# Expert rows gathered as two half rows, one by token and one by slot, the second a tile later

## The reference

```
idx = ...                                   # (tokens, 8, 16) chosen by two top-k over product keys
g = jax.nn.softmax(top_s, axis=-1)
u = expert_down[idx]
act = jax.nn.gelu(jnp.einsum('thkd,td->thk', u, xb).astype(f32), approximate=False)
return jnp.einsum('thk,thkd->td', (g * act).astype(xb.dtype), expert_up[idx])
```

## Time and profile before

| | us |
|---|---|
| median of 3 runs | 4412.91 |
| lowest and highest run | 4394.77, 4413.0 |
| span of the profiled execution | 4384.4 |
| start of the first gather in it | 1435.3 |
| start of the last tile's copy of rows | 3969.1 |

### The profile page before, as it was taken

The page is one execution under the profiler, slowest core; times in us unless marked ns, Lnnn a source line. Parts: engine busy times, 40 slices in busy tenths (PEclk is TensorE's granted clock), DMA queues, the critical chain, the costliest instruction groups (busy, mean ns, idle before and its releaser), DMA issues.

```text
span 4384.4 us, 39661 instructions
## 1 busy us (share of the span) xinstructions
PE 3487.9 (80%) x11633; PEld 1922.7 (44%) x11633; DVE 2354.8 (54%) x4730; ACT 1050.6 (24%) x3019; POOL 1348.0 (31%) x1232
## 2 busy tenths in 40 slices
PE   7699996469997687786787788778769778877876
PEld 1698774135555342352353344335325324324432
DVE  0651111746663767457546646646755755664574
ACT  1110112123341222222222222222222222222222
POOL 0020110400000343344444443434444444443442
PEclk9799997689998898898899889889889889988988
DMA  7232210642323899999999999999999999999996
GB/s 273 69 103 110 82 61 31 246 165 86 101 72 134 345 374 374 381 384 366 361 389 368 376 375 379 366 370 380 382 384 378 381 374 383 377 375 375 395 382 272
DMA packets 210634, 1269.30 MB, mean 290 GB/s; under 512 B 25875, under 2 KB 51099, under 8 KB 74060
## 3 DMA queue, kind: packets, MB, share of 16 engines
q0 software_dynamic: 159504, 1114.68, 64.3%
q1 hardware_dynamic: 50902, 152.03, 9.9%
HBM read 1218.26 MB, written 48.36 MB: 289 GB/s over the span
## 4 chain that ended last, share of the span: by engine, by line
DMA 26%; PE 25%; issue 8%; ACT 4%; POOL 3%; DVE 3%; POOLq 0%; ACTq 0%; DVEq 0%; SPq 0%
DMA e_buf<-in_experts,e_idx 26%; PE ps L1771 22%; PE ps L1502 3%; POOL e_buf L1738 3%; DVE e_buf L1840 2%; ACT e_wts L1812 2%; ACT e_diag L1816 1%; ACT e_acts L1810 1%; DMA e_buf<-in_experts,e_idxT 0%; DMA r_wq<-in_w_query 0%; POOLq L58 0%; DVE r_work L1590 0%; DVE r_row L1591 0%; DVE r_work L1587 0%; DVE r_pos L1550 0%
## 5 line engine op out<-in xcount | busy, mean ns | idle before, releaser
L1771 PE MATMUL ps<-e_buf,e_diag 128*128 128x512 f32 x4096 | 2026.0, 652 | 638.7 <-ACT e_diag L1816 635.2
L1840 DVE SCALAR_TENSOR_TENSOR e_buf<-e_buf,e_h 128x1024 f32<-128x1024 f32 x1024 | 1248.2, 1227 | 1091.6 <-DMA e_buf<-in_experts,e_idx 1075.2
L1738 POOL DMA_INDIRECT e_buf<-in_experts,e_idx x1024 | 1195.4, 1167 | 1605.1 <-PE ps L1771 1406.3
L1771 PEld LDWEIGHTS ps<-e_buf,e_diag 128*128 128x128 f32 x4096 | 836.0, 210 | 1758.4 <-issue 990.9
L1810 ACT ACTIVATE e_acts<-e_dots 128x4 f32<-128x4 f32 x256 | 52.6, 205 | 2085.0 <-DVE e_buf L1840 2076.4
L1816 ACT ACTIVATE e_diag<-ident,e_wts 128x128 f32<-128x128 f32 x1024 | 327.3, 390 | 27.8 <-ACT e_wts L1812 2.7
L1502 PEld LDWEIGHTS ps<-r_h2T,r_wq 128*128 128x128 f32 x2304 | 269.3, 193 | 34.0 <-issue 34.0
L1502 PE MATMUL ps<-r_h2T,r_wq 128*128 128x128 f32 x2304 | 269.9, 276 | 3.1 <-DMA r_wq<-in_w_query 3.1
L830 PE MATMUL ps<-xo_w_out,xo_catT 128*128 128x512 f32 x512 | 224.5, 592 | 1.7 <-DVE xo_x L863 1.7
L1812 ACT ACTIVATE e_wts<-e_acts,e_gate 128x1 f32<-128x1 f32 x1024 | 218.5, 284 | 9.2 <-ACT e_acts L1810 1.1
L74 PE MATMUL ps<-p_wth,hT_high 128*128 128x512 f32 (+1 forms) x432 | 170.6, 395 | 10.9 <-PEq L413 10.9
(11 more groups left out here) (338 smaller groups left out, 3007.2 us busy)
## 6 DMA issues: line engine op xcount, KB each, us to landing
w_mod_sb<-in_w_mod SPq DMA_DIRECT2D x12, 2048.0 KB, 8.4
e_buf<-in_experts,e_idx POOLq DMA_INDIRECT x1024, 9.1
p_wt<-in_w_rows SPq DMA_DIRECT2D x6, 2048.0 KB
proj_d<-p_ev POOLq DMA_DIRECT2D x48, 256.0 KB, 2.3
x_zgv<-proj_d SPq DMA_DIRECT2D x8, 1536.0 KB
p_w<-in_w_chan SPq DMA_DIRECT2D x20, 512.0 KB, 4.3
r_wq<-in_w_query SPq DMA_DIRECT2D x4, 2048.0 KB, 20.2
xbc_d<-p_res POOLq DMA_DIRECT2D x12, 516.0 KB, 3.0
```

Of the source, the lines that this page charges most:

```text
L1738: return pool.indirect_dma_start(out=buf[s][:], out_offset=None, in_=io["experts"], in_offset=bass.IndirectOffsetOnAxis(ap=numbers, axis=0 ...
L1771: last = nc.tensor.matmul(g.bank(cols), diag[:, k % RING, :], buf[k % RING][:, D + cols * 512:D + (cols + 1) * 512], start=(k == 0), stop= ...
L1840: V.scalar_tensor_tensor(out=down, in0=down, scalar=1.0, in1=row, op0=ALU.mult, op1=ALU.mult, accum_out=out).then_inc(sem, 1)
```

## The change

The table `experts` becomes two tables, `expert_down` and `expert_up`, with rows of 4 KB. Each is fetched by its own gathers.

The down rows are fetched as before, a slot of 128 tokens at a time, into 7 buffers of 4 KB a partition. VectorE's dot is the same; a down buffer is free when its dot has ended.

The up rows are fetched a tile later and the other way round: one gather for each token, whose 128 slots lie on partitions. For this TensorE turns the indices and the gates of a tile (`turn_route`), VectorE copies them out (`keep_route`), TensorE turns the activations of the last tile (`turn_acts`), and VectorE multiplies gates and activations into `wz` (`weigh`), a zeroed tensor in which the weights of token t stand in column 32 t + 31, so that 32 neighbouring columns hold one token's weights at the right place and zeros elsewhere. TensorE then sums a token over partitions with 32 columns of weights (`add_up`). Four tokens of a group go to the four column groups of 32 (PSUM partitions 0, 32, 64, 96), two products of 512 columns for each. One signal `summed` a group frees its four buffers; there are 8 up buffers.

ScalarE's scaling and its diagonals go; it makes one gelu for half a tile. GpSimd issues down gather k of tile n and up gather k of tile n-1 in turn. So the first tile has down gathers alone, and a ninth turn has up gathers alone, with the 8 down and 8 up gathers of the sample rows. The finish of a tile comes two tiles after its dots. The loops over tiles are written out, the pieces of the routing are moved two groups later, and the waits on GpSimd are no longer kept apart with a nop of their own, except a few. Some constants of the phases before are freed to make room. The core of the diff:

```diff
-    def tensor(self, pe, n):
+    def tensor(self, pe, n, turned_kept=()):
 
         g, nc = self.g, self.g.nc
         pe.wait_ge(self.h2_in, n * 16 + 16)
+        for kept, count in zip(turned_kept, (n, n, n - 1)):
+            if count:
+                pe.wait_ge(kept, count)
...
+            if n and half == 0:
+                dve.wait_ge(route_ps, n)
...
-            V.tensor_copy(self.idx[:, ks], self.num[:, ks]).then_inc(self.numbered, 1)
+            V.tensor_copy(self.idx[n % 2][:, ks], self.num[:, ks]).then_inc(self.numbered, 1)
...
-PE_PIECES = {q: 1 for q in range(1, 14)}
-ACT_PIECES = {q: 1 for q in (2, 4, 6, 7, 9, 10, 12, 13, 14, 18, 26)}
-DVE_PIECES = {8: 2, 9: 3, 11: 2, 12: 3, 13: 2, 14: 2, 15: 2, 16: 2, 17: 4, 19: 4, 20: 4, 21: 3, 22: 3, 23: 3,
-              24: 3, 25: 3, 27: 1}
-
-FIRST_ACT_PIECES = {6: 1}
+PE_PIECES = {q: 1 for q in range(3, 16)}
+ACT_PIECES = {q: 1 for q in (4, 6, 8, 9, 11, 12, 14, 15, 16, 20, 28)}
+DVE_PIECES = {10: 2, 11: 3, 12: 2, 13: 3, 14: 2, 15: 2, 16: 2, 17: 2, 18: 2, 19: 4, 20: 4, 21: 4, 22: 3, 23: 3,
+              24: 3, 25: 3, 26: 3, 28: 1}
+
+FIRST_ACT_PIECES = {3: 1}
...
+        down = [sb(f"down{s}", [P, D]) for s in range(ND)]
+        up = [sb(f"up{s}", [P, D]) for s in range(NU)]
+        h2 = sb("h2", [P, D])
+        dots, acts = [sb(f"dots{b}", [P, SLOTS]) for b in range(2)], sb("acts", [P, SLOTS])
+        idxT, gateT = [sb(f"idxT{b}", [P, P], U32) for b in range(2)], [sb(f"gateT{b}", [P, P]) for b in range(2)]
+        wz = sb("wz", [P, Q * (P + 1)])
...
+            for n in range(NT):
                 sp.wait_ge(h2_kept, n + 1)
-                sp.dma_start(rt.h2[:], g.h2_d[bass.ds(n * P + P, P), :]).then_inc(rt.h2_in, 16)
-                if not first:
-                    store_y(n - 1)
-                sp.dma_start(fin.x1[:], g.x1_d[bass.ds(n * P, P), :]).then_inc(fin.x1_in, 16)
-
-            tile(0, True)
-            with sp.Fori(1, NT) as n:
-                tile(n, False)
+                sp.dma_start(rt.h2[:], g.h2_d[(n + 1) * P:(n + 2) * P, :]).then_inc(rt.h2_in, 16)
+                if n == 1:
+                    load_x1(0)
+                if n >= 2:
+                    store_y(n - 2)
+                    load_x1(n - 1)
...
+            def take_down(i, numbers):
+                if i >= ND:
+                    pool.wait_ge(dotted, i - ND + 1)
+                take(down[i % ND], "expert_down", numbers, down_in[i % ND])
+
+            def take_up(i, numbers):
+                if i >= NU:
+                    pool.wait_ge(summed, (i - NU) // GROUP + 1)
+                take(up[i % NU], "expert_up", numbers, up_in[i % NU])
+
+            nc.gpsimd.memset(wz[:], 0.0).then_inc(wz_clear, 1)
+            for n in range(NT + 1):
                 for k in range(SLOTS):
-                    wait_apart(pool, summed, n * SLOTS + k + 1)
-                    if k in (0, HALF_SLOTS - RING):
-
-                        half = 0 if k == 0 else 1
-                        ks = slice(half * HALF_SLOTS, (half + 1) * HALF_SLOTS)
-                        wait_apart(pool, rt.numbered, n * 2 + half + 1)
-                        nc.gpsimd.tensor_copy(idx[:, ks], rt.idx[:, ks]).then_inc(idx_kept, 1)
-                        wait_apart(pool, idx_kept, n * 2 + half + 1)
-                    gather(k % RING, idx[:, k:k + 1]).then_inc(landed[k % RING], 16)
-
-            with pool.Fori(0, NT) as n:
-                tile(n)
-            pool.wait_ge(idxT_ready, 1)
+                    if n < NT:
+                        if k in (0, SLOTS // 2):
+                            wait_apart(pool, rt.numbered, n * 2 + (1 if k == 0 else 2))
+                        take_down(n * SLOTS + k, rt.idx[n % 2][:, k:k + 1])
+                    elif k < NS:
+                        if k == 0:
+                            wait_apart(pool, idxT_ready, NT + 1)
+                        take_down(n * SLOTS + k, idxT[NT % 2][:, k:k + 1])
+                    if n > 0:
+                        if k == 0:
+                            wait_apart(pool, idxT_ready, n)
+                        t = Q * (k % GROUP) + k // GROUP
+                        take_up((n - 1) * SLOTS + k, idxT[(n - 1) % 2][:, t:t + 1])
             for b in range(NS):
-                wait_apart(pool, summed, NT * SLOTS + b + 1)
-                gather(b % RING, idxT[:, b:b + 1]).then_inc(landed[b % RING], 16)
+                take_up(NT * SLOTS + b, idxT[NT % 2][:, b:b + 1])
...
-            def tile(n, first):
-                route = rt.tensor(pe, n + 1)
-                for k in range(SLOTS):
-                    if k == 0 and not first:
-                        pe.wait_ge(fin.sum_read, n)
-                    pe.wait_ge(weighed, n * SLOTS + k + 1)
-                    for cols in range(2):
-                        last = nc.tensor.matmul(g.bank(cols), diag[:, k % RING, :],
-                                                buf[k % RING][:, D + cols * 512:D + (cols + 1) * 512],
-                                                start=(k == 0), stop=(k == SLOTS - 1))
-                    last.then_inc(summed, 1)
-                    if k % GROUP == GROUP - 1:
-                        drive(route, PE_PIECES.get(k // GROUP, 0))
+            def turn_acts(n):
+                pe.wait_ge(acted, 2 * n + 2)
+                pe.wait_ge(gateT_ready, n + 2)
+                nc.tensor.transpose(g.bank(2, cols=P), acts[:], g.ident[:]).then_inc(acts_ps, 1)
+
+            def turn_route(n):
+                rs = rows_of(n)
+                pe.wait_ge(rt.gated, 2 * n + 2)
+                if n > 1:
+                    pe.wait_ge(weighed, n - 1)
+                for m, src in enumerate((rt.num, rt.gate)):
+                    last = nc.tensor.transpose(turned(m, rs), src[0:rs, :], g.ident[0:rs, 0:rs])
+                last.then_inc(route_ps, 1)
+
+            def add_up(n, j):
+                for c in range(GROUP):
+                    i = n * SLOTS + j * GROUP + c
+                    pe.wait_ge(up_in[i % NU], 16 * (i // NU) + 16)
+                for half in range(2):
+                    for c in range(GROUP):
+                        at = Q - 1 + Q * (Q * c + j) - j
+                        last = nc.tensor.matmul(g.ps[Q * c:Q * (c + 1), half * 512:(half + 1) * 512],
+                                                wz[:, at:at + Q],
+                                                up[(n * SLOTS + j * GROUP + c) % NU][:, half * 512:(half + 1) * 512],
+                                                start=(j == 0), stop=(j == Q - 1))
+                last.then_inc(summed, 1)
+
+            for n in range(NT + 1):
+                turn_route(n)
+                if n:
+                    turn_acts(n - 1)
+                    pe.wait_ge(weighed, n)
+                    if n > 1:
+                        pe.wait_ge(fin.sum_read, n - 1)
+                if n < NT:
+                    route = rt.tensor(pe, n + 1, (idxT_ready, gateT_ready, weighed))
+                for q in range(NG):
+                    if n:
+                        add_up(n - 1, q)
+                    if n < NT:
+                        drive(route, PE_PIECES.get(q, 0))
...
+            def gelu(n, half):
+                ks = slice(half * (SLOTS // 2), (half + 1) * (SLOTS // 2))
+                act.wait_ge(dotted, n * SLOTS + ks.stop)
+                if n and half == 0:
+                    act.wait_ge(acts_ps, n)
+                A(acts[:, ks], dots[n % 2][:, ks], ACT.Gelu).then_inc(acted, 1)
...
+            def keep_route(n):
+                rs = rows_of(n)
+                dve.wait_ge(route_ps, n + 1)
+                V.tensor_copy(idxT[n % 2][:, 0:rs], turned(0, rs)).then_inc(idxT_ready, 1)
+                V.tensor_copy(gateT[n % 2][:, 0:rs], turned(1, rs)).then_inc(gateT_ready, 1)
+            def weigh(n):
+                dve.wait_ge(acts_ps, n + 1)
+                dve.wait_ge(gateT_ready, n + 1)
+                if n:
+                    dve.wait_ge(summed, n * NG)
+                else:
+                    dve.wait_ge(wz_clear, 1)
+                cols = wz[:].rearrange("p (t m) -> p t m", m=Q)[:, 0:P, Q - 1:Q].squeeze(2)
+                V.tensor_tensor(cols, g.bank(2, cols=P), gateT[n % 2][:], ALU.mult).then_inc(weighed, 1)
...
+                if n:
+                    keep_route(n)
                 for k in range(SLOTS):
+                    q = k // GROUP
+                    if k == 1 and n:
+                        weigh(n - 1)
+                    dot(n * SLOTS + k, h2[:], dots[n % 2][:, k:k + 1])
                     if k % GROUP == GROUP - 1:
+                        if n == 0:
+                            drive(own, FIRST_DVE_PIECES.get(q, 0))
+                            if q == 7:
+                                keep_route(0)
+                        if q == 1 and n >= 2:
+                            fin.add(dve, n - 2, P)
+                        if q == 4 and n >= 2:
+                            fin.scale(dve, n - 2, P)
...
```

(32 more changed lines are left out.)

158 lines of the change are left out of this document (58 added, 100 removed).

## The result

| | before | after |
|---|---|---|
| median of the runs, us | 4408.1 | 4510.57 |
| lowest to highest, us | 4394.77 to 4413.0 | 4502.2 to 4532.42 |
| span of the profiled execution, us | 4384.4 | 4506.5 |
| GpSimd (POOL) busy | 31% | 53% |
| TensorE (PE) busy | 80% | 53% |

The ratio after/before is 1.0257, with a 95% interval of 1.0223 to 1.0291 (the two medians of the table alone give 1.0232): slower, and the time is the one that was forecast. The parts of the sum are near too, but one reason behind them was wrong.

What follows compares the result with a forecast made beforehand. The expert stage was taken as close to DMA-bound. Head 1435, first tile 262, seven full tiles of 360, last stretch 236 and end 28 make 4481 us; plus 28.5 from span to median, 4510, range 4390 to 4680.

Steps and rivals of the forecast that it cites:

- a first and a last stretch: Ends of the expert stage: first tile 262 us with down gathers alone, last stretch 236 us with up and sample gathers.
- The limit of a full tile: Full tile: DMA, not GpSimd, was taken as the limit, giving 360 us, bounds 340 and 386.
- DMA's 351 + 8 = 359: Full tile: 340 us of transfer at share 0.97 makes 351, plus 8 of idle DMA at the tile's start.
- The rival: Full tiles: GpSimd's issuing becomes the bound at the earlier mean gather, 376 us a tile, time 4622; chance 0.14.
- two gathers per dot fit: GpSimd beside VectorE's dots: with dots every 2.65 us, two gathers fit per dot, if barely.
- the rival's point of decision: Full tiles: GpSimd as the bound decides from a mean gather of 1.10 us up, with 0.30 between.
- DMA's own price: Expert stage: 395 GB/s while a queue runs, so 340 us of transfer in a 362 us tile, 22 us missing.
- Start of each tile: Up gathers wait for the last tile's sums to be read; DMA runs dry 8 us per tile, bounds 0 and 15.
- The 24 us from the last dot until GpSimd goes on: Tile start: last sum 4.5, transposes and copies 4, eight dots 10, read 1.2, first group 4.5 us.
- TensorE's group: Sum of four tokens, 16 passes in four column groups: 4.5 us, between 1.8 at full overlap and 7.1 at none.
- Last stretch: Tile 7's up gathers and the sample gathers alone, paced by two buffer groups: 236 us, bounds 203 and 277.
- the queue never runs dry: Full tiles: buffers freed sooner keep DMA at share 1.0, 340 us a tile, time 4336; chance 0.14.

Runs made afterwards that it cites:

- Half rows: Changed kernel with each gather fetching only the first 2 KB of a 4 KB row, the rest left out: 4599.46 us, ratio 1.0467.
- the row in PSUM: Changed kernel with the token row that VectorE's dots read put in two PSUM banks instead of SBUF: 4367.36 us, ratio 0.9936.
- by twos: Kernel before with ScalarE's gelu, scaling and diagonals after every two dots instead of four: 4097.01 us, ratio 0.9333.
- early read: Changed kernel with VectorE's read of the finished sums moved from behind a tile's eighth dot to behind its first: 4445.22 us, ratio 1.011.
- long ring: Changed kernel with three sets of four up buffers instead of two in the last stretch, using free down buffers: 4455.25 us, ratio 1.0161.
- one column group: Changed kernel with all four tokens of a group on the same 32 PSUM rows, so output rows differ: 4799.54 us, ratio 1.0924.
- all three corrections: Changed kernel with the dots' token row in PSUM, sums read earlier in a tile, and three up-buffer sets in the last stretch: 4264.68 us, ratio 0.9709.
- before with two gathers: Kernel before with two tables and two gathers of 4 KB rows per slot into halves of the same buffer: 4461.34 us, ratio 1.0166.

## Why the prediction was right, and where it was not

- **Direction and size.** Slower, because a first and a last stretch are added and the full tiles give next to nothing back (14 us in all was put). Both held: 264.5 us and 270.9 for the ends, and 362 for a full tile, which was 362 before.
- **The limit of a full tile: the step that failed** is "I therefore take DMA, not GpSimd, as the limit". DMA's 351 + 8 = 359 stood for GpSimd's 346 + 11 = 357. The rival had the mechanism and too high a price, since it took the mean of before, 1.167 us: in a full tile of after it is 1.04 to 1.08. The reason given for the step, that two gathers per dot fit and that a VectorE which is behind "also keeps up", holds only where VectorE makes dots alone (one gather every 1.25 us, 410 GB/s); where routing lies between the dots it is one every 1.43 us and 377 GB/s. And the rival's point of decision, 1.10, was set against the forecast of 360 without the wait at the tile's start. With the 11 us, 256 x (m + 0.30) + 11 = 360 from m = 1.06. Half rows (no gain from half the bytes) and the row in PSUM (a gain with all the bytes) show the limit from both sides.
- **DMA's own price** failed too. "395 GB/s while a queue runs" is bytes over the DMA share, and was taken as a ceiling. It was a rate at 3.2 gathers in flight: the same rows go at 418 by twos, 4 KB rows at 407. So 340 us was not the floor of a tile of before: it can go in 325, and lost at least 37 us to late buffers, not 22. Nor is the share a measure of the rate: in the first tile of after it was 0.76 where 0.65 was put, for the same bytes in nearly the same time (258 GB/s).
- **Start of each tile.** 8 us of idle DMA were put. DMA loses some 7 us there (shares 0.58 and 0.04 of two times 5 us above), but GpSimd stands 10.8 us, and that counts where GpSimd paces the tile. The 24 us from the last dot until GpSimd goes on were 27 (2051 to 2078.25), with errors that partly cancel: the eight dots took 17 us (2055.84 to 2073.07) where 10 was put, because most of them wait for their rows, and the sums and the turning took less. The early read shows that the wait for the sums is the cause, as the working had it.
- **TensorE's group.** 4.5 us put, 3.64 found: the term was mis-sized in both of its parts. The overlap is nearly full, 1.92 us at the higher clock level (granted 1.00 from 4300.4 to 4302.4 in the long ring) against 7.03 in one column group, 3.7 times; and the clock is at the lower one for most groups (granted 0.65 in a tile, 0.50 in the group at 2051, 2.4 and 1.2 GHz being the levels). The Trainium skill's page "TensorEngine Tiling (Array Packing)", section "Theoretical Speedup", gives up to 4 times; the long ring's 1.92 us agrees.
- **Last stretch.** 14.1 us per two groups put, 14.1 found as the mean of four loops (14.47 in the rows below), with two errors that cancel: the sum 3.64 instead of 4.5, and landing 5.84 instead of 4.2, because half the bytes did not take 1.2 us off the landing of the earlier trace rows. The long ring shows that the stretch was bound by this loop, as the working had it.

One loop of it (timeline of after; sum, release, the fourth issue, next sum):

```profile
4268.79 3.64 PE L1807 MATMUL ps<-e_up,e_wz 128*32 128x512 f32 x16 [6.57 <-DMA e_up<-in_expert_up,e_idxT]
4272.73 0.94 POOL L1750 DMA_INDIRECT e_up<-in_expert_up,e_idxT  x1 [3.27 <-PE ps L1807]
4276.48 0.94 POOL L1750 DMA_INDIRECT e_up<-in_expert_up,e_idxT  x1 [0.30 <-issue]
4283.26 3.64 PE L1807 MATMUL ps<-e_up,e_wz 128*32 128x512 f32 x16 [5.59 <-DMA e_up<-in_expert_up,e_idxT]
```

From 4268.79: sum 3.64, release 0.30, issues to 4277.42, then 5.84 until the next sum.

- **The rival "the queue never runs dry"** (340 us a tile, 4336) is what the row in PSUM nearly gives, 343 us and 4367, still with the two added stretches.

- **A side remark**, that unrolling lengthens the code that is fetched, was wrong: the page's two queues of kind "instruction" moved 2.59 MB before and 1.74 MB after.

What stays open: why half rows lengthen the up gathers and not the down gathers, and what bounds the full tiles of all three corrections (334 us), where GpSimd still waits 205 us for dots and 119 for sums while DMA is at 407 GB/s.

## What to carry to other kernels

A DMA share near 1 doesn't say that DMA is the limit: compare the rate in GB/s with that of a stretch that has more transfers queued, or free the buffers earlier and look. Before a gather is split in two, count its issues, 1.24 us each here at best, and look at what else holds up the engine that issues them, in the stretch where it is held up most and not on the average. And when buffers are freed in groups, try smaller groups before moving the work: half the group gave 6.7% here with no other change.

## What the runs showed of the hardware that was not expected

- A gather of 128 rows takes GpSimd the same time whatever the rows hold: the median is 0.946 us for 8 KB and for 4 KB rows, and 0.953 for the down gathers of 2 KB rows, with 0.30 us to the next at best. (The up gathers of 2 KB rows have 1.280, held up by dots.)
- Moving half the bytes made the kernel slower (4599 us for 4511).
- In full tiles a DMA share near 1 stood beside very different rates: 0.97 beside 364 GB/s (before with two gathers, 2181 to 2551), 0.98 beside 379 (after), 1.02 beside 407 (all three corrections), 1.01 beside 423 (by twos, 1759 to 2085).
- One input of the dot in PSUM leaves the dot as long as it was (1.22 us), and takes 0.12 us off the mean gather beside it.
- In the long ring's last stretch, groups of 16 passes alternate between 1.92 us, after 1.72 us of idle TensorE, and 3.40 us, after 3.20 us of it; the granted clock is 1.00 in the one (4300.4 to 4302.4), 0.56 in the other (4305.5 to 4309), and 0.83 in the mean (4280 to 4420).
